# Layers written out, the work between two layers put into one stage by token halves, and stick-breaking attention with the keys on the partitions

## The reference

```python
h_res = _layer_norm(x, ln_in_g, ln_in_b)
for l in range(DEPTH):                                   # DEPTH = 2
    proj = jnp.einsum('bsd,dc->bsc', h_res, w_in[l])
    ...
    log_f = jax.nn.log_sigmoid((f_logit + b_forget[l]).astype(jnp.float32))
    f_cum = jnp.cumsum(log_f, axis=1).transpose(0, 2, 1)
    out_fox = _causal_softmax_attention(..., head_scale, f_cum)
    out_sb = _stick_breaking_attention(...)
    out_mla = _causal_softmax_attention(...)
    ...                                                  # out_mem: softmax over 256 memory rows
    mixed = jnp.concatenate([_merge(out_fox), _merge(out_sb), _merge(out_mla), _merge(out_mem)], axis=-1)
    y = jnp.einsum('bsc,cd->bsd', mixed * jax.nn.silu(gate), w_out[l])
    h_res = _layer_norm(DEEPNORM_ALPHA * h_res + y, ln_g[l], ln_b[l])

def _stick_breaking_attention(q, k, v, scale):           # 4 heads of 64 channels
        valid = key_pos[None, :] < q_pos[:, None]
        z = jnp.einsum('bhqd,bhkd->bhqk', qb, k).astype(jnp.float32) * scale
        log_keep = jnp.where(valid, jax.nn.log_sigmoid(-z), 0.0)
        log_tail = lax.cumsum(log_keep, axis=3, reverse=True) - log_keep
        w = jnp.where(valid, jnp.exp(jax.nn.log_sigmoid(z) + log_tail), 0.0)
        return jnp.einsum('bhqk,bhkd->bhqd', w.astype(v.dtype), v)
```

## Time and profile before

| | us |
|---|---|
| median of 3 runs (4813.99 to 4831.76) | 4828.31 |
| profiled execution, its own time | 4825.18 |
| span of that execution, first to last instruction | 4823.3 |
| first block in it, to the first instruction of the second | about 1962.6 |
| PE busy in the span | 4020.0 (83%) |
| DVE busy in the span | 1814.7 (38%) |

### The profile page before, as it was taken

How to read it: one execution, slowest core, us unless ns; L and a number is a source line. 1 busy time by engine, 2 the same in 40 slices (tenths; PEclk the granted TensorE clock), 3 DMA queues, 4 the chain that set the end, 5 groups by cost and what they waited for, 6 DMA issues and landing times. The chain is left out here.

```text
span 4823.3 us, 66417 instructions
## 1 busy us (share of the span) xinstructions
PE 4020.0 (83%) x28894; PEld 2817.2 (58%) x28894; DVE 1814.7 (38%) x3012; ACT 1169.7 (24%) x2221; POOL 556.5 (12%) x181
## 2 busy tenths in 40 slices
PE   2887888948768888569976999999799994999996
PEld 2664657936645678134753555555566543878875
DVE  6438164254372452220283443444301105232232
ACT  2326143023252330010052333333200002010010
POOL 2210002221100021100110000000000001232231
PEclk9999889979988999789987999999899996999998
DMA  3100001111000111521001000000210001111121
GB/s 120 45 27 1 8 18 44 71 66 44 27 8 1 36 36 71 212 94 35 9 1 55 20 16 16 21 16 7 66 73 29 11 24 61 53 43 43 52 71 61
DMA packets 138349, 206.67 MB, mean 43 GB/s; under 512 B 4214, under 2 KB 104336, under 8 KB 136472
## 3 DMA queue, kind: packets, MB, share of 16 engines
q1 hardware_dynamic: 138056, 202.61, 12.4%
q10 hardware_dynamic: 16, 0.00, 0.0%
HBM read 179.50 MB, written 23.10 MB: 42 GB/s over the span
## 5 line engine op out<-in xcount | busy, mean ns | idle before, releaser
L2505 PE MATMUL banks<-h_channel_major,pair_weights 128*128 128x512 f32 x768 | 392.5, 627 | 0.3 <-ACT x_residual L2896 0.3
L205 PE MATMUL banks<-h_high,weights_high 128*128 128x512 f32 x640 | 252.0, 394 | 44.2 <-PEq L221 39.1
L205 PE MATMUL banks<-h_low,weights_high 128*128 128x512 f32 x640 | 251.2, 393 | 0.0
L205 PE MATMUL banks<-h_high,weights_low 128*128 128x512 f32 x640 | 251.0, 392 | 0.0
L190 POOL CAST weights_high<-weights_value 128x2048 fp32r<-128x2048 f32 (+1 forms) x36 | 67.8, 1884 | 1504.5 <-DMA weights_value<-in_w_in_dram 904.8
L205 PE MATMUL banks<-h_high,ffn_weights_high 128*128 128x512 f32 x512 | 204.4, 399 | 33.8 <-PEq L75 33.8
L849 PE MATMUL banks<-keys,queries 64*128 64x256 f32 (+7 forms) x512 | 140.5, 546 | 91.4 <-ACT attention_scratch L953 70.1
L205 PE MATMUL banks<-h_low,ffn_weights_high 128*128 128x512 f32 x512 | 203.8, 398 | 0.0
L205 PE MATMUL banks<-h_high,ffn_weights_low 128*128 128x512 f32 x512 | 203.6, 398 | 0.0
L205 PE MATMUL banks<-ffn_weights_high,hidden_high 128*128 128x512 f32 x512 | 199.5, 390 | 3.1 <-ACT hidden_value L3277 3.1
L205 PE MATMUL banks<-ffn_weights_high,hidden_low 128*128 128x512 f32 x512 | 199.2, 389 | 0.0
(11 more groups left out here) (419 smaller groups left out, 8641.3 us busy)
## 6 DMA issues: line engine op xcount, KB each, us to landing
ffn_weights_value<-in_w_ff_dram SPq DMA_DIRECT2D x32, 1024.0 KB, 5.4
weights_value<-in_w_in_dram SPq DMA_DIRECT2D x26, 1024.0 KB, 5.3
ada_weights<-in_ada_w_dram SPq DMA_DIRECT2D x12, 2048.0 KB, 8.2
pair_weights<-in_w_in_dram SPq DMA_DIRECT2D x24, 512.0 KB, 4.1
x_waiting<-x_residual SPq DMA_DIRECT2D x2, 4096.0 KB, 16.8
weights_value<-in_w_out_dram SPq DMA_DIRECT2D x8, 1024.0 KB, 5.1
h_value<-x_waiting SPq DMA_DIRECT2D x2, 4096.0 KB, 12.5
x_waiting_two<-x_residual SPq DMA_DIRECT2D x2, 4096.0 KB, 18.5
```

Of the source, the lines that this page charges most:

```text
L205: mm = nc.tensor.matmul(out, x, y, start=(first and i == 0 and j == 0), stop=(last and i == n - 1 and j == 2))
L2505: mm = nc.tensor.matmul(bank, wr[:, n % R_TILES, c, :], k.ht[:, c, half * HALF:(half + 1) * HALF], start=(c == 0), stop=(c == KT - 1))
```

## The change

- **The loop is gone.** `first_block` writes both layers out; the residual lies in `x_residual` in one and in a second tensor in the other, so that an output product can read one while the next layer's input is made in the other.
- **`boundary`** takes the place of the start, `norm_x`, `norm_mem`, the memory's turning, `turn_x`, `fox_project`, the clearing stage, `out_project` and `norm_out`. It is called three times: at the start (load, norm, turn, project), between the layers (output product, norm, turn, project) and at the end (output product, norm). The output product runs by halves of the tokens (tiles 0 to 3, then 4 to 7), for which all four chunks of output weights are resident: two of them get buffers of their own over `values` and `attention_scratch`. The norm is two DVE instructions for each tile (subtract the mean and multiply by the gain; multiply by the inverse root and add the bias); ACT and POOL take no part. PE's transposes of the first half stand among the last output groups of the second half, and those of the second half among the projection groups of the first. Output and projection groups now share 4 PSUM banks. DVE takes the low part straight from PSUM. The forget sums go to DRAM and back inside this stage. The forget weights are 32 columns wide, not 128.
- **`stick_attention`** takes the place of `attention_stage`. Units are two heads, half of the queries (512 or fewer columns) and one tile of 128 keys: 24 units, of which 12 are 512 columns wide, and 4 each are 384, 256 and 128. The keys lie on the partitions, the sum over later keys inside a tile is a matmul with a triangular matrix of -1 (`minus_later`) into the bank that already holds the scores, which PE computes twice, and earlier sums are folded in by multiplying the total by exp(-sum of this tile). Transposes, copies and the scan are gone.
- **`gate`** loads output chunks 2 and 3 first and POOL splits five chunks in it, not three; each sigmoid has a place of its own. `sb_project` has no zero padding.

The diff, cut to what is spoken of:

```diff
-            def stick_logs(u):
...
-                chain(dve, nc.vector.scalar_tensor_tensor(z[:, 0:n], scores(u), 0.0, z[:, 0:n], ALU.max, ALU.add))
-                chain(dve, nc.vector.tensor_tensor(z[:, n - P:n], z[:, n - P:n], k.before01[:], ALU.mult))
-                chain(dve, nc.vector.tensor_tensor_scan(buf.cum[:, 0:n][:, ::-1], k.one[:, 0:1].broadcast_to([P, n]),
-                                                        z[:, 0:n][:, ::-1], 0.0, ALU.mult, ALU.add))
-                chain(dve, nc.vector.tensor_tensor(z[:, 0:n], scores(u), buf.cum[:, 0:n], ALU.subtract))
-                nc.vector.tensor_tensor(z[:, n - P:n], z[:, n - P:n], k.before_add[:], ALU.add).then_inc(log_ready, 1)
...
+            def products(u, to, stop):
+                p, half, b = units[u]
+                for e in range(2):
+                    mm = nc.tensor.matmul(to[:, e, :], kt[half_rows[e], p, b * P:(b + 1) * P],
+                                          qt[half_rows[e], p, half * HALF + first[u]:(half + 1) * HALF], start=True, stop=stop)
+                return mm
...
-                        mm = nc.tensor.matmul(scores(u, at, at + size), q(h, g, t), key(h, g, a, a + size), start=True, stop=True)
...
-                        mm = nc.tensor.transpose(k.psum[:, 4 + p % turn_banks, (i % 4) * P:(i % 4 + 1) * P],
-                                                 weights[u % NW][:, i * P:(i + 1) * P], k.ident[:])
...
+                if u >= 2:
+                    pe.wait_ge(softplus_ready, u - 1)
+                products(u, z(u), True).then_inc(scores_done, 1)
...
+            def do_tails(u):
+                if u:
+                    pe.wait_ge(weights_ready, u)
+                products(u, logs(u), False)
+                pe.wait_ge(softplus_ready, u + 1)
+                for e in range(2):
+                    mm = nc.tensor.matmul(logs(u)[:, e, :], k.minus_later, part(sp_bufs, u)[:, e, :], start=False, stop=True)
+                mm.then_inc(tails, 1)
+                if u:
+                    pe.wait_ge(kept_ready, u)
+                for e in range(2):
+                    mm = nc.tensor.matmul(k.psum[half_rows[e], 6, first[u]:HALF], k.one[:, 0:1].broadcast_to([P, 64]),
+                                          part(sp_bufs, u)[:, e, :], start=True, stop=True)
+                mm.then_inc(block_summed, 1)
             def do_sum(u):
...
+                p, half, b = units[u]
+                pe.wait_ge(weights_ready, u + 1)
+                if u:
+                    pe.wait_ge(added, u)
+                for e in range(2):
+                    mm = nc.tensor.matmul(k.psum[half_rows[e], 7, first[u]:HALF], values(2 * p + e, b), part(p_bufs, u)[:, e, :],
+                                          start=True, stop=True)
+                mm.then_inc(summed, 1)
...
             def exponent(u):
...
+                act.wait_ge(tails, u + 1)
+                if diagonal[u]:
+                    act.wait_ge(diagonal_ready, n_diagonal[u])
                 if u >= 2:
                     act.wait_ge(summed, u - 1)
...
+                nc.scalar.activation(part(p_bufs, u), logs(u), ACT.Exp).then_inc(weights_ready, 1)
...
+            def keep(u):
+                act.wait_ge(block_summed, u + 1)
...
+                nc.scalar.activation(keep_bufs[u % 2][:, first[u]:HALF], k.psum[:, 6, first[u]:HALF], ACT.Exp,
+                                     scale=-1.0).then_inc(kept_ready, 1)
...
+            for it in range(N + 1):
+                if it < N:
+                    softplus_log(it)
+                if it >= 1:
+                    exponent(it - 1)
+                    keep(it - 1)
...
+            def softplus(u):
...
+                ins = nc.vector.scalar_tensor_tensor(sp, z(u), 0.0, part(z_bufs, u), ALU.max, ALU.add)
...
+                    ins = nc.vector.tensor_tensor(own, own, k.before01.unsqueeze(1).broadcast_to([P, 2, P]), ALU.mult)
+                ins.then_inc(softplus_ready, 1)
...
+            def mask_diagonal(u):
+                dve.wait_ge(tails, u + 1)
+                own = logs(u, first[u], first[u] + P)
+                nc.vector.tensor_tensor(own, own, k.before_add.unsqueeze(1).broadcast_to([P, 2, P]),
+                                        ALU.add).then_inc(diagonal_ready, 1)
...
+            def add(u):
...
+                    nc.vector.tensor_tensor(acc, acc, keep_bufs[u % 2][:, first[u]:HALF], ALU.mult).then_inc(faded, 1)
+                    dve.wait_ge(faded, faded_before[u])
+                    dve.wait_ge(summed, u + 1)
+                    nc.vector.tensor_tensor(acc, acc, k.psum[:, 7, first[u]:HALF], ALU.add).then_inc(added, 1)
...
+            for it in range(N + 2):
+                if it < N:
+                    softplus(it)
+                if it >= 2:
+                    add(it - 2)
+                if it < N and diagonal[it]:
+                    mask_diagonal(it)
...
+SLOT_OF = {C_FL: 4, C_FQ: 0, C_FK: 1, C_FV: 3, C_OUT + 2: 2, C_OUT + 3: 3}
...
+        for n, b in enumerate(layers):
+            boundary(k, a, layers[n - 1] if n else None, b)
+            first_layer(k, a, b)
+        boundary(k, a, layers[-1], None)
...
+                    sp.wait_ge(products, 20)
+                    W.load(sp, C_FQ)
+                    sp.wait_ge(products, 24)
+                    W.load(sp, C_FK)
+                    sp.wait_ge(products, 32)
+                    W.load(sp, C_FV)
+                for half in range(2):
+                    sp.wait_ge(normed, 4 * half + 4)
...
+                c, t = out_group(g)
+                if g < 16 and g % 4 == 0 and c == 1:
+                    pe.wait_ge(w_split, 1)
+                room(g)
...
+                pe.wait_ge(split, 8 if n < 9 else 16)
...
+            for g in range(n_out):
+                if b and 22 <= g < 30:
+                    do_turn(0, g - 22)
+                do_out(g)
+            if b:
+                if not last:
+                    for c in range(KT):
+                        do_turn(0, c)
+                for n in range(9):
+                    if n >= 4:
+                        do_turn(1, n - 4)
+                    do_fox(n)
+                for c in range(5, KT):
+                    do_turn(1, c)
+                for n in range(9, 18):
+                    if mem and n == 14:
+                        do_mem()
+                    do_fox(n)
...
+            def norm(t):
...
+                step(nc.vector.scalar_tensor_tensor(row, row, k.moments[:, t, 0:1], gain, ALU.subtract, ALU.mult))
+                nc.vector.scalar_tensor_tensor(row, row, k.root[:, t:t + 1], bias, ALU.mult, ALU.add).then_inc(normed, 1)
...
+            def low(half, c):
...
+                dve.wait_ge(rounded, n + 1)
+                nc.vector.tensor_tensor(b.h_low[:, c, s], k.bank(4 + n % 4), b.h_high[:, c, s], ALU.subtract).then_inc(split, 1)
...
+            if last:
+                for g in range(n_out):
+                    add(g)
+                    if g == 16:
+                        moments(0)
+                    if g == 17:
+                        invert_root(0)
+                    if 17 <= g < 21:
+                        norm(g - 17)
+                    if b and 23 <= g < 31:
+                        low(0, g - 23)
...
+                    if half == 0:
+                        moments(0)
+                        invert_root(0)
+                        for t in range(4):
+                            norm(t)
+                        for c in range(KT):
+                            low(0, c)
+            moments(1)
+            invert_root(1)
+            for t in range(4, 8):
+                norm(t)
+            if mem:
+                norm_mem()
```

940 lines of the change are left out of this document (449 added, 491 removed).

## The result

The changed kernel takes 4604.9 us (median of 4 runs), the kernel before 4824.4 us (median of 4 runs): a ratio of 0.9543, 95% interval 0.9519 to 0.9567. The forecast was 4586 us, in a range from 4535 to 4660. The profiled execution took 4605.16 us with a span of 4603.4 us, 219.9 us less than the span before; the forecast had 239. Each ratio in this document is to the kernel before, timed anew beside the kernel in question.

The account below looks back on a forecast made before the run. It took DVE's chain to bound stick-breaking before and PE after, with PE the bound almost throughout between the layers. Gains 86 + 70 + 2 + 29 + 52 = 239 us; 4825 - 239 = 4586 us, range 4535 to 4660.

Parts of the forecast that it names:

- The unit's 5.7 us: Stick-breaking: PE's work in a full unit takes about 5.7 us, 103 us for 18 full units a layer.
- the 12 us I took: Stick-breaking's start: 12 us beyond the work, because POOL's splits block DVE's masks.
- one DVE instruction passes between two of POOL's, and the fourth tile is ready at 38: Start of the program: POOL's splits block DVE's norms, so the fourth tile is ready at 38 us, not 23.
- where I had 2 each: Gates: POOL now has five splits and ends later than PE, costing 2 us in each layer.
- four banks are a margin: Between the layers: DVE's statistics push it over PE's pace for four groups, but four banks give 11 us of margin.
- the sum of 181: Between the layers: PE's output product, projections and transposes, 174.6 us, plus three times 2 us; gain 70 us.
- PE without gaps over 2 us: Sign of being right: no longer PE gap between the layers, from the first output group to the last projection.
- the 46 us in front of it: End of the block: 46 us of norm stage become 13, plus 2 to 4 for gate and stage end; gain 29.
- The forget sums: They come back during projections instead of in the next stage; 1 us gained in each layer, 2 in all.
- The likeliest case: Whole kernel: the forecast itself, 4586 us, chance 0.57.
- The rival with a packed start (4553): Splits don't block the norm or PE packs tighter: start ends at 118, stick-breaking near 112 us; 4553 us, chance 0.17.
- that with turns between the engines (4642): Stick-breaking: single log bank, path over four engines and mode changes leave gaps; stage 150 us, total 4642, chance 0.2.

Follow-up runs that it names:

- experiment 4: Changed kernel with the tile's sum of stick-breaking computed for one column only, ACT still working the full width; 4597.1 us (one run).
- experiment 2: Changed kernel with POOL's four splits at the start begun only after the norms of the first four tiles; 4594.1 us, ratio 0.9522.
- experiment 3: Changed kernel with the gate's last two splits of output weights moved to the start of the output product; 4601.1 us, ratio 0.9536.
- experiment 9: Changed kernel with an unused tile of 384 bytes in front of the first block's tiles; 4596.3 us (one run).
- experiment 11: Kernel of experiment 7 with first-half transposes back in place, POOL's stick-breaking splits after the fifth unit's softplus, and 384 unused bytes; 4565.4 us, ratio 0.9472.
- experiment 7: Changed kernel with later POOL splits at start and boundary, three splits in the gate, earlier memory-norm root, first-half transposes one group later; 4575.7 us, ratio 0.9485.
- experiment 5: Changed kernel with stick-breaking's second scores brought by DVE into the bank of the logs instead of computed by PE; 4622.6 us, ratio 0.9584.

## Why the prediction was right, and where it fell short

**Stick-breaking: right, and the sum with some luck.** 86.6 us for 86. The unit's 5.7 us came, and PE as the bound of full units (experiment 4). Two deviations cancel. The stage took 118.9 us where I had 122: the start was 3 us cheaper than the 12 us I took, since DVE's masks met only the end of POOL's longer instruction. And the second layer's stage, which I took to be like the first's, was 2.7 us shorter before (168.1 against 170.8), so that the gains are 44.6 and 42.0 us. The Trainium skill (TensorEngine Tiling, Key Properties) says that a change of the tiling mode drains the array. The rows of the unit bound what that costs here. Inside a group the matmuls, or pairs of them side by side, start 0.43 us apart. The two steps of the tile's sum, behind which the form stays the same (128*64), take 0.91 us, 0.05 more than two such steps; the four steps of the scores and of the triangular product, behind which the form changes, take 1.92 and 1.91 us, 0.2 more than four. The unit's 12 steps make 5.16 us of 5.69, so all changes together cost at most some 0.5 us a unit. My groups were measured from start to start and had held them.

**The start: mechanism right, size 5 us short.** The step that failed was "one DVE instruction passes between two of POOL's, and the fourth tile is ready at 38". It was ready at 41.1, because POOL's own instructions became longer as well, 2.88 and 5.35 us where 1.89 and 4.5 to 4.6 are usual, so that a tile took 8.27 us and not POOL's undisturbed 6.4 to 6.8. Experiment 2 shows that this was avoidable. The Trainium skill (SBUF — State Buffer, Who interferes with whom) says that a VectorE instruction with two SBUF inputs contends with a GpSimd instruction that reads SBUF, and one with at most one doesn't. The trace agrees: the norm waited, while in experiment 2 the statistics (one input, 5.78 us for eight) and the low parts, which read PSUM (0.69 us), ran at full speed beside POOL's splits.

**The gates: 5.2 and 6.8 us lost where I had 2 each.** (From the gate's first matmul to the output product's, 91.5 us in both layers became 96.7 and 98.3.) I had looked at when POOL ends, not at what it does to DVE on the way. Its last two splits stand beside DVE's last groups, whose instructions on two SBUF tiles took up to 5.1 us. Without these splits 4.4 and 4.7 us came back in experiment 3, and 4.5 and 4.7 us between experiments 9 and 11, which both have the unused bytes. It is the same mechanism that I had used at the start and in stick-breaking. The rest, 0.8 and 2.2 us, is the place of the operands: experiment 9 gave 0.7 and 2.1 us of it back.

**Between the layers: 65.8 us for 72.** The term "four banks are a margin" held: no addition was late. Four terms were missing from the sum of 181 or too small in it. First, the output product begins at the clock's half level, 1.2 GHz: its first two groups took 5.26 and 3.18 us instead of 2.86, 2.7 us. I had reckoned every group at 2.88. The first 6.2 us of the output product, in the kernel before and in the changed one:

```profile
879.80:886.00 6.20, 6.20 (x39) 6.20 (x40) 0.00 (x0) 0.00 (x0) 5.18 (x2) 0.72 0.94 349
792.10:798.30 6.20, 6.20 (x30) 6.20 (x31) 0.00 (x0) 1.23 (x1) 6.12 (x2) 0.52 0.81 292
```

The kernel before had a slow start too, behind a wait of 4.2 us: its first group took 4.44 us. That the changed kernel's is slower because its wait is longer (8.6 us) isn't shown. In experiment 9, behind 8.8 and 8.9 us, the first group took 4.3 us; in the second layer of experiment 7, behind 4.2 us, the first two took 5.26 and 3.13.

Second, POOL's split of the queries' weights met the last norm of the first half, and PE waited for it. ("PE without gaps over 2 us" was a sign that I had named; this gap is longer.)

```profile
857.73 2.79 DVE L1190 SCALAR_TENSOR_TENSOR second_value<-second_value,norm_root,h_channel_major 128x1024 f32<-128x1024 f32 x1
```
```profile
860.58 0.66 PE L1100 MATMUL banks<-masks_and_identity,second_value 128*128 128x128 f32 x4 [2.71 <-DVE second_value L1190]
```

Third, the ten groups of 512 columns came after 5.58 us each and not 5.44, 1.4 us together (the place of the operands, experiment 9), and fourth, the transposes cost 6.8 us where I took 5. These are 8.6 us, and the stretch is 6.7 us longer than the sum had it without the gate (185.7 for 179); which terms were some 2 us too large stays open. The loop's end is no gain beside this: it lies in the 251 us that the sum was set against.

**The end: 26.7 us instead of 31.** The norm's tail is the forecast's: DVE ends 13 us after PE's last matmul starts. But I took the 46 us in front of it from the stretch between the layers, which holds the loop's end; in the second layer the kernel before needed 43.7 us from PE's last matmul to the next stage's first DMA issue (1918.9 to 1962.6). The changed kernel needs 16.7 (1730.6 to 1747.4), so that the change of stage takes 3.8 us and not 2. The slow start of the output product is 0.5 us longer than before (4.94 against 4.44 us for the first group).

**The forget sums: nothing, where I had 2.** Forget attention starts no earlier against its own end: 147.0 and 147.7 us to stick-breaking, as before.

**The rivals.** The likeliest case came, with four of its terms (start, gates, boundary, end) 4 to 6.5 us too good. More than half of that were waits that begin when one engine's work is put beside another's (5 at the start, 5 in the gates, 2.7 at the boundary); no instruction was miscounted. That the error of the whole is 19 us and not 23.5 is luck: the untouched second half ran 4.4 us shorter. The rival with a packed start (4553) is out, that with turns between the engines (4642) too, though experiments 4 and 5 show its mechanism in the narrow units.

## What to carry to other kernels

Where two engines get in each other's way, list every place at which their work now stands side by side, not only those that the trace before shows: here one mechanism, reckoned with at two places and not at the two others, made some 8 of the 23.5 us by which the first block missed the forecast. A piece of work off the critical path can be put behind the work that it would block with one wait, as long as what stands behind it in its own queue isn't needed sooner (17.6 us at the start for two small edits). When the bound of a stage is named, ask for which of its units: taking work from PE helped the full ones and not the diagonal ones.

## What the runs showed of the hardware

- The place of operands in SBUF moves the pace of matmuls: 0.2267, 0.2288 and 0.2325 us from one 512-column matmul of the projections to the next, with the same instructions; 384 bytes decided it. For 256 columns the place that was better for 512 was slightly worse in the first layer (2.88 against 2.86 us for 24). Which bytes collide with which stays open.
- When DVE and POOL block one another they take turns, and both pay: a DVE instruction of 1.28 us took up to 5.40 us at the start, ending 1.08 us behind POOL's; POOL's cast took 2.88 us instead of 1.89, its subtraction 5.35 instead of 4.5.
- Behind PE's wait in front of the output product the first groups ran partly at the half clock, in every run. The cost didn't follow the wait's length: 1.5 to 2.7 us behind waits of 4.2 us (1.5 in the kernel before), 1.3 to 2.8 us behind waits of 8.2 to 8.9 us.
- The same attention in front of the gate took 36.8 to 38.2 us or 39.4 to 39.5 us, by whether the granted clock fell to its half level once more in it.
